# Four of eight weight-row sums of a transformer kernel moved from VectorE to GpSimd, with the load order of the ring changed to fit

## The reference, cut to what matters

```python
mod = silu(c) @ w_ada + b_ada                  # 1 x 1024 times 1024 x 6144
sh1, sc1, ga1, sh2, sc2, ga2 = split(mod, 6)
q, k, v, z, xbc, dt_raw, gates = split((rmsnorm(x, g) * (1 + sc1) + sh1) @ w_in)
s = q @ k.T * scale + bias                     # 16 heads, local and context keys
p = softmax(s); o = p @ v
```

## Time and profile before

| | |
|---|---|
| median of 3 runs | 2247.09 us |
| profiled execution, its time | 2250.94 us |
| profiled execution, its span | 2249.2 us |
| busy: TensorE, VectorE, ScalarE, GpSimd | 82%, 43%, 33%, 8% of the span |
| chain that ended last | TensorE 56%, DMA 37%, VectorE 3%, ScalarE 2% |

### The profile page before, as it was taken

One profiled execution on the slowest core, in us unless ns is written; L12 is line 12 of the kernel. 1 busy time (PEld: TensorE's weight loads), 2 busy tenths in 40 slices (PEclk: granted clock), 3 DMA queues, 4 the chain that ended last, 5 costly groups with the idle time before them and its releaser, 6 DMA issues.

```text
span 2249.2 us, 26826 instructions
## 1 busy us (share of the span) xinstructions
PE 1839.1 (82%) x10746; PEld 1172.2 (52%) x10746; DVE 961.9 (43%) x1677; ACT 750.4 (33%) x1294; POOL 180.7 (8%) x183
## 2 busy tenths in 40 slices
PE   7998999999987565656565556656999999989999
PEld 5865778789952111111111111112957888768887
DVE  5677887876640000000000000002657747787745
ACT  4343567776321000000000000003355535665533
POOL 1200122252011000000000000000000000420000
PEclk9999999999988878787878888788999999999999
DMA  8544233345699999999999999998524564324562
GB/s 328 220 158 170 97 130 123 114 151 192 240 401 426 428 428 427 429 428 428 428 429 428 428 429 429 428 428 337 186 87 161 187 234 156 136 89 170 186 238 95
DMA packets 68167, 619.08 MB, mean 275 GB/s; under 512 B 8272, under 2 KB 17232, under 8 KB 22624
## 3 DMA queue, kind: packets, MB, share of 16 engines
q1 hardware_dynamic: 56320, 598.84, 65.8%
q10 hardware_dynamic: 9392, 10.63, 1.7%
q0 software_dynamic: 2352, 8.19, 1.1%
HBM read 616.52 MB, written 1.11 MB: 275 GB/s over the span
## 4 chain that ended last, share of the span: by engine, by line
PE 56%; DMA 37%; DVE 3%; ACT 2%; issue 1%; POOL 0%; SPq 0%; DVEq 0%; ACTq 0%; POOLq 0%
DMA ring<-in_w_edown 18%; DMA ring<-in_w_eup 17%; PE bank L540 10%; PE bank L542 10%; PE bank L541 10%; PE bank L2999 5%; PE bank L3001 3%; PE bank L2791 2%; PE bank L2808 2%; PE bank L3442 1%; PE bank L1942 1%; DMA ring<-in_w_ada 1%; DMA ring<-in_w_in_x 1%; PE bank L1367 1%; PE bank L1275 1%
## 5 line engine op out<-in xcount | busy, mean ns | idle before, releaser
L2895 DVE TENSOR_TENSOR work<-bank,work 128x512 f32<-128x512 f32 x14 | 9.7, 692 | 799.6 <-PE bank L2791 799.6
L508 DVE TENSOR_TENSOR ring_parts<-ring,ring_parts 128x2048 fp32r<-128x2048 f32 (+2 forms) x125 | 281.8, 2259 | 144.4 <-ACT ring_parts L502 144.1
L502 ACT CAST ring_parts<-ring 128x2048 fp32r<-128x2048 f32 (+3 forms) x151 | 276.4, 1835 | 180.8 <-DMA ring<-in_w_mlp_out 81.6
L2791 PE MATMUL bank<-ring,work 128*32 128x512 f32 x1024 | 172.3, 808 | 127.4 <-DMA ring<-in_w_egate 67.3
L2808 PE MATMUL bank<-ring,work 128*32 128x512 f32 x1020 | 172.6, 808 | 104.1 <-DMA ring<-in_w_edown 98.0
L2791 PE MATMUL bank<-work 128*32 128x512 f32 x1024 | 152.2, 724 | 93.7 <-DMA work<-in_w_eup 66.0
L540 PE MATMUL bank<-hT_hi,ring_parts 128*128 128x256 f32 (+2 forms) x584 | 196.8, 337 | 0.5 <-issue 0.3
L542 PE MATMUL bank<-hT_hi,ring_parts 128*128 128x256 f32 (+2 forms) x584 | 187.4, 321 | 0.0
L541 PE MATMUL bank<-hT_lo,ring_parts 128*128 128x256 f32 (+2 forms) x584 | 187.3, 321 | 0.0
L2999 PE MATMUL bank<-hn_parts,ring_parts 128*128 128x512 f32 x512 | 181.6, 400 | 0.0
L2791 PEld LDWEIGHTS bank<-ring,work 128*32 128x32 f32 x1024 | 34.1, 130 | 258.2 <-issue 108.0
(11 more groups left out here) (483 smaller groups left out, 3552.3 us busy)
## 6 DMA issues: line engine op xcount, KB each, us to landing
ring<-in_w_edown SPq DMA_DIRECT2D x62, 2048.0 KB, 26.0
work<-in_w_eup SPq DMA_DIRECT2D x33, 2048.0 KB, 27.3
ring<-in_w_egate SPq DMA_DIRECT2D x33, 2048.0 KB, 26.0
work<-in_w_egate SPq DMA_DIRECT2D x31, 2048.0 KB, 25.9
ring<-in_w_eup SPq DMA_DIRECT2D x31, 2048.0 KB, 26.0
ring<-in_w_mlp_in SPq DMA_DIRECT2D x32, 1024.0 KB, 4.8
ring<-in_w_mlp_out SPq DMA_DIRECT2D x30, 1024.0 KB, 4.8
ring<-in_w_ada SPq DMA_DIRECT2D x12, 2048.0 KB, 9.3
```

The costliest lines, as they stand in the source:

```text
L502: act.copy(halves_of(name, ring_parts)[1], halves_of(name, ring)[0]).then_inc(hi_made, 1)
L508: dve.tensor_tensor(lo, halves_of(name, ring)[0], hi, ALU.subtract).then_inc(lo_made, 1)
L2791: last = pe.matmul(bank[which][32 * n:32 * n + 32, :], rows[:, 2 * c + k2, :], w[:, k2, 512 * n:512 * n + 512], start=c == 0 and k2 == 0, ...
```

## The change

Sets 6, 7, 10 and 11 are summed by GpSimd (`POOLED`). `ada_products_pool` multiplies the 8 tiles of a set in place in the ring, each by its scalar, broadcast along the tile (8 TENSOR_TENSOR of 128x512). `ada_total_pool` adds them as a tree of 4, 2 and 1 (7 TENSOR_TENSOR), the last into `set_sum`, and releases the slot. VectorE keeps sets 4, 5, 8 and 9. In the ring, sets 10 and 11 move from behind `v1` and `dt` to behind `xs0_0`. TensorE's and ScalarE's orders are as before.

```diff
-        ADA_AFTER = {"v0": (4, 5), "k1": (6, 7), "v1": (8, 9, 10), "dt": (11,)}
+        ADA_AFTER = {"v0": (4, 5), "k1": (6, 7), "v1": (8, 9), "xs0_0": (10, 11)}
...
+        POOLED = (6, 7, 10, 11)
+        ada_pooled = sem("ada_pooled")
+
         def ada_chunk(i):
-            chunk(f"ada{i}", d["w_ada"][0, i], KT, 512, (ada_ready, i + 1))
+            done = (ada_pooled, POOLED.index(i) + 1) if i in POOLED else (ada_ready, i + 1 - sum(p < i for p in POOLED))
+            chunk(f"ada{i}", d["w_ada"][0, i], KT, 512, done)
...
+        def ada_products_pool(pool, i):
+            link = stepper(pool, pool_step)
+            w = slot(f"ada{i}")
+            wait_chunk(pool, f"ada{i}")
+            for k in range(KT):
+                s = sT[:, k, 2 * ADA_SET - 2:2 * ADA_SET - 1].broadcast_to([P, 512])
+                last = pool.tensor_tensor(w[:, k, :], w[:, k, :], s, ALU.mult)
+            link(last)
+
+        def ada_total_pool(pool, i):
+            link = stepper(pool, pool_step)
+            w = slot(f"ada{i}")
+            for n in (4, 2):
+                for k in range(n):
+                    last = pool.tensor_tensor(w[:, k, :], w[:, k, :], w[:, k + n, :], ALU.add)
+                link(last)
+            pool.tensor_tensor(set_sum[i - ADA_FIRST], w[:, 0, :], w[:, 1, :], ALU.add).then_inc(ada_pooled, 1)
...
-            if 7 <= step < 15:
-                ada_sum(dve, 6, step - 7, step - 6)
-            if step == 22:
-                ada_sum(dve, 7)
...
-            ada_sum(dve, 10)
...
-            if step in sums:
-                ada_sum(dve, 11, sums[step], sums[step] + 2)
```

More of the change, by code:

```diff
@@ L383, in feature_chunks @@
                 chunk(f"{name}_{u}", w[0, first + u], KT, 256, (gemm_ready, group + 2 * u + 2), f"{name}_{u}" != "aq_0")
+                for i in ADA_AFTER.get(f"{name}_{u}", ()):
+                    ada_chunk(i)
         def token_chunks(name, w, h, group_end):
@@ L401, in build @@
         narrow_chunk("dt", d["w_in_dt"][0, 0], 2 * SSD_HEADS, GROUP["dt"] + 1)
-        for i in ADA_AFTER["dt"]:
-            ada_chunk(i)
         for g in range(SSD_G):
@@ L1081, in ada_sum @@
                     dve.scalar_tensor_tensor(total, w[:, k, :], s, total, ALU.mult, ALU.add).then_inc(ada_ready, 1)
+        def ada_products_pool(pool, i):
[14 more added lines that the diff above has]
+            pool.tensor_tensor(set_sum[i - ADA_FIRST], w[:, 0, :], w[:, 1, :], ALU.add).then_inc(ada_pooled, 1)
         def ada_rows_pe(pe):
-            pe.wait_ge(ada_ready, ADA_FIRST + 2 * ADA_SET)
+            pe.wait_ge(ada_ready, ADA_FIRST + 2 * ADA_SET - len(POOLED))
+            pe.wait_ge(ada_pooled, len(POOLED))
             pe.wait_ge(acs_done, 1)
@@ L1678, in ssd_ahead_dve @@
             splits = {2: "xs0_0", 12: "xs0_1"}
-            sums = {4: 0, 6: 2, 9: 4, 10: 6}
             if step in splits:
@@ L4151, in _ @@
             ada_pool(pool)
-            na_bias_pool(pool, 0, 0, 8)
-            na_bias_pool(pool, 1, 0, BIASES)
-            end_stage(pool, "pool")
-            na_bias_pool(pool, 1, BIASES, 8)
+            na_bias_pool(pool, 0, 0, 7)
+            ada_products_pool(pool, 6)
+            ada_total_pool(pool, 6)
+            na_bias_pool(pool, 0, 7, 8)
+            na_bias_pool(pool, 1, 0, 1)
+            ada_products_pool(pool, 7)
+            na_bias_pool(pool, 1, 1, 3)
+            ada_total_pool(pool, 7)
+            na_bias_pool(pool, 1, 3, BIASES)
+            end_stage(pool, "pool")
+            ada_products_pool(pool, 10)
+            na_bias_pool(pool, 1, BIASES, 7)
+            ada_total_pool(pool, 10)
+            na_bias_pool(pool, 1, 7, 8)
+            ada_products_pool(pool, 11)
+            ada_total_pool(pool, 11)
             end_stage(pool, "pool")
```

## The result

The changed kernel takes 2267.16 us (median of 4 runs, 2263.81 to 2268.94) against 2247.08 for the kernel before beside it: 1.0091 of its time, 95% interval 1.0078 to 1.0103. The forecast was 2245.6, with a range up to 2252. The profiled execution is the fastest of the four: 2263.81 us with a span of 2262.0, so 12.8 us longer than the span before. The profiled execution of before was 3.9 us above its own median, of which 2.8 lie ahead of the first half (TensorE's first scores start at 94.00 now and started at 96.76).

What follows compares the result with a forecast made beforehand. TensorE and the experts' DMAs bound most of the chain; the change targeted TensorE's hole between the halves, the wait for `xs0_0`. Terms -6.1 + 4.0 + 0.4 + 0.2 = -1.5 from 2247.09 gave 2245.6 us, range 2240 to 2252.

Steps and rivals of the forecast that it cites:

- GpSimd beside VectorE: Tail of the second half: ten VectorE instructions each 0.4 us slower beside GpSimd; +4.0 us, between 1.0 and 9.0.
- The load order: Between the halves: `xs0_0` issued ahead of sets 10 and 11 lands earlier; -6.1 us, between -7.5 and -4.5.
- VectorE's sums: Both halves: the 22.9 us of sums leaving VectorE gain nothing; 0, between -1.5 and 0.
- The first half: Table 7 behind set 6 on GpSimd delays a bias, GpSimd's price there is hidden; +0.2 us, bounds 0 to 2.
- The test that I had named: First half: the forecast fails if TensorE idles over 2 us more there.
- Rival B: Second half's tail: each of ten VectorE instructions waits a whole GpSimd instruction, 12.9 us; +7.3, 2254.4 us; chance 0.10.
- The bias tables and later loads: Second half: table 15 behind set 10 costs +0.4 us, bounds 0 to 3; later loads such as `xs0_1` 0, at most 1.5.
- Rival C: Second barrier: GpSimd, at 1.7 us an instruction, ends late and holds ScalarE and VectorE; about +4, 2251 us; chance 0.08.

Runs made afterwards that it cites:

- e2_first: Kernel before with only sets 6 and 7 summed by GpSimd, in the old ring order: 2256.86 us, ratio 1.0050.
- e3_second: Kernel before with only sets 10 and 11 summed by GpSimd, in the new ring order: 2254.16 us, ratio 1.0034.
- e1_order: Kernel before with only the new ring order; all sums stay on VectorE, sets 10 and 11 summed later: 2241.12 us, ratio 0.9979.
- e4_no_sums: Changed kernel without GpSimd's products and first six additions of each set; queues, waits and releases stay: 2241.13 us, ratio 0.9971.
- e5_linked: Changed kernel with GpSimd waiting on its own semaphore after every product and addition: 2252.69 us, ratio 1.0031.
- e8_scalar: Changed kernel with GpSimd's products taking a scalar per partition in place of a second tensor: 2248.56 us, ratio 1.0013.
- e9_both: Changed kernel with both a semaphore wait after every GpSimd instruction and products taking a scalar per partition: 2254.03 us, ratio 1.0029.

## Why the prediction was wrong, point by point

The step that failed is the price of GpSimd beside VectorE. It was put at nothing in the first half and at 0.4 us for each of ten instructions in the second. The runs show 9.9 and 13.0 us (`e2_first` against before, `e3_second` against `e1_order`).

- **The load order, -6.1: right.** From `v1_1`'s release to the scores it is 10.2 us (189.57 to 199.78), where it was 16.4 (183.21 to 199.63): -6.2. The ring order alone gave 5.8 us in the median.
- **VectorE's sums, 0: right.** The medians of `e4_no_sums` and `e1_order` differ by 0.01 us; that they come so near is luck, but nothing above some 2 us is there.
- **The first half, +0.2 with bounds 0 to 2 (for the bias tables; GpSimd's arithmetic at nothing): wrong, the step that failed first.** It cost 9.1 us: from the first scores to `v1_1`'s release it was 86.45 (96.76 to 183.21) and is 95.57; `e2_first` gives +9.0 in the table. I took VectorE's idle 14.8 us and TensorE's filler for cover. That cover doesn't hold against a delay of 4.33 (4.81 less 0.48), behind which TensorE stood for 2.54 us and again, for the rotary embedding, for 2.71. Nor does it quite hold against turns alone: TensorE stood 2.01 us at 114.67 behind a row of them, and 2.12 us at the same place in `e5_linked`. That idle time would also bring the clock down was in no term. The test that I had named, over 2 us more of idle TensorE in the first half, came out against the forecast.
- **GpSimd beside VectorE, +4.0 with bounds 1 to 9: wrong in mechanism and size.** `e3_second`'s second half is 15.4 us longer than that of its twin `e1_order`: 10.9 us of idle time and 4.5 of busy time. The latter can't be put down to GpSimd, for before, without its sums, is busy as long (38.93 us, `e3_second` 38.88). In the medians it is 13.0. I counted ten instructions, each late by less than one of GpSimd's. `e5_linked` shows that turns alone already cost more than my 0.4 each, and the changed kernel adds waits through whole rows. The price came from the mild medians of rows 8. The same trace had the turns in plain sight, in a place that I had not read. Here GpSimd's splits L519, eight to a weight with no wait between them in the code, run beside six accumulations of VectorE (L3949), five inside the row and one behind it:

```profile
1939.07 12.68 POOL L519 TENSOR_TENSOR ring_parts<-ring,ring_parts 128x512 fp32r<-128x512 f32 x10
...
L3949 DVE SCALAR_TENSOR_TENSOR work<-work x6: 352/1245/1257, 1945.5 to 1951.9; 128x128 f32<-128x128 f32 x6
```

  An instruction of 0.35 us takes 1.25, a whole one of GpSimd's. But none waits longer, though the row is 12.7 us long. So before's trace could have given the turns, and could not have given the starving: a long row without a pause is not enough for it.
- **Rival B, strict turns, 2254.4 with a chance of 0.10:** its mechanism is what `e5_linked` does when turns are all that is left. That `e5_linked` measured 2252.69 is in part luck: B charged the tail alone, and 1.29 us for each instruction, while the run loses 3.9 us already in the first half (90.35 from the first scores to `v1_1`'s release, 86.45 in `e1_order`), and its L1889 loses 0.83. The forecast should have given turns most of the weight, and a case above them for waits longer than an instruction.
- **The bias tables and later loads, +0.4 and 0: no cost seen**, in `e4_no_sums` and in the changed kernel's trace, where no bias waits for its table. Rival C did not happen in the changed kernel (GpSimd's last sum ended at 239.2, 15.8 us ahead of its next work); it needed the slower products of `e8_scalar` and `e9_both`.
- **The sum.** In the profiles, -2.8 at the start, +9.1, -6.2, +11.9 and +0.7 behind the stage make the +12.8 of the span. The forecast was for the medians, where it is +20.1; the 7.2 us between the two are the distances of the two profiled executions from their medians, and, apart from the 2.8 at the start, no trace here says where in the kernel they lie.

The rule of the Trainium skill that I had set aside ("SBUF — State Buffer", § SBUF: two separate sides: an exclusive lock, held for the whole instruction) was nearer than my reading. The traces agree that the holder keeps it for a whole instruction: beside the split L512 an addition of GpSimd (at 230.45) took 3.34 us, its longest, instead of 1.25. They go beyond it for the loser, which waits through up to 25 instructions, where the rule speaks of one. With single waits the prediction had made it rival B.

Still open: why VectorE sometimes gets its turn within a row and sometimes starves. In the changed kernel's first row of products, from 110.39, one instruction after the other took about 1.26 us; in the last, from 219.64, the same line was held for 7.38. In before, rows of L519 gave turns only. No run here tells what decides it. That `e1_order`'s second half is 3.8 us shorter than before's in the two profiles is the clock: its idle time is 0.7 us longer (4.69 against 3.96), its busy time 4.5 shorter, at a granted clock of 1.00 against 0.88. Its second block of 16 products L1367 in the tail, for one, takes 1.95 us, where before's and the changed kernel's take 3.68. Open is why the clock fell in one execution and not in the other: the idle 2.57 us ahead of that block are the same in both, and `e2_first`, with before's load order, was at 0.96 there. In the medians `e1_order` gains 5.8 us, no more than the term, so the 3.8 may belong to the one execution that was profiled.

## What to carry to other kernels

Work that an engine does in the shade of another costs nothing there, so first show, by leaving it out, that moving it could gain anything (here nothing above 2 us). Price arithmetic on GpSimd beside VectorE's SBUF-only work by what was measured here: a turn costs up to a whole instruction of GpSimd's, and at worst the wait lasts as long as the row that GpSimd issues without a pause. Look for the first in the trace before, where VectorE and GpSimd already meet. If it must be, one-tensor products (18.6 us back) or pauses (14.5) help, not both together, and so does VectorE work that is not held: the accumulating form, or what reads PSUM (which no run here tried as a remedy). None of them came down to the 2241.12 of leaving the sums on VectorE. And where a wait leaves TensorE idle, count the slower clock behind it. When a small reordering rides along with a larger move, measure it alone: it was the whole gain.

## What the runs showed of the hardware that I had not expected

- A VectorE instruction without a PSUM operand was held by a row of GpSimd instructions for 4.81, 6.02, 7.38 and, with instructions of 0.36 us, 9.24 us, and each time it ended 0.29 us after the instruction at which the row paused for a semaphore.
- Not in every long row: in before, beside eight unpaused L519, VectorE's L3949 paid one instruction of GpSimd's each time (1.25 for 0.35 us) and never more.
- Never held: L1313 and L1401 (PSUM operand, 0.68 and 0.41 us beside running products), the accumulating form of the scaling (0.75 against 0.48 us of the plain form alone), and the one reciprocal L1893 of `e5_linked` (1.75, as alone), though it reads only SBUF.
- GpSimd's product with a scalar per partition takes at least 1.55 us, with a broadcast tensor at least 1.03, and yet the kernel is 18.6 us faster with the first.
- The wait stands in the record as busy time of the waiting engine: VectorE was busy 85% of the second half (46.46 of 54.60), and the chain called it "issue".
- TensorE stood idle for 5.3 us in two pieces from 146.5 us on, and its granted clock was 0.50 from 151 to 157 us, where it had been 1.00 from 145 to 151 and was 0.95 in the 8 us after; `e2_first` shows the same from 150 to 159 us.
